# A two-layer hybrid decoder step on one core: constants split in two, the samples' last products reordered, identity products placed in waits

## The reference, cut to what matters

```python
def trunk(x, states, hist_valid, weights):
    for layer in range(DEPTH):          # DEPTH = 2
        if layer % 2 == 0:
            h, dconv, delta, pool = delta_pool_mixer(x, ...)   # "mixer 0"
        else:
            h, lconv, lru = rglru_mixer(x, ...)                # "mixer 1", the second mixer
        x = layer_norm(ALPHA * x + h, ln_mix_g[layer], ln_mix_b[layer])
        f = moe(x, router_w, router_bias, moe_w_gate[layer], moe_w_up[layer], moe_w_down[layer])
        x = layer_norm(ALPHA * x + f, ln_ffn_g[layer], ln_ffn_b[layer])

def gated_delta_rule(q, k, v, g, beta, s0):   # per head, in chunks of C rows
    m = jnp.where(strict, jnp.einsum('bhnid,bhnjd->bhnij', kb, k) * decay, 0.0)
    tinv = jnp.eye(C) - m;  power = -m
    for _ in range(max((C - 1).bit_length() - 1, 0)):
        power = power @ power
        tinv = tinv + tinv @ power
    ...
    # o = q_dec @ s + a_intra @ u_new,  s = s * exp(g_last) + k_dec^T @ u_new

# then: o = o * rsqrt(mean(o*o) + eps) * norm_w * silu(z);  y = concat(o, pooled) @ w_out
```

## Time and profile before

| | us |
|---|---|
| median of 3 runs | 1407.63 (1405.7 to 1408.05) |
| profiled execution | 1408.48 |
| its span, first to last instruction | 1406.7 |
| TensorE busy | 1244.5 (88%) |
| VectorE busy | 968.3 (69%) |
| ScalarE busy | 730.8 (52%) |
| GpSimdE busy | 183.6 (13%) |
| mean granted clock of TensorE | 0.935 |

### The profile page before, as it was taken

How to read it: one execution, slowest core, us unless ns; L and a number is a source line. 1 busy time by engine, 2 the same in 40 slices (tenths; PEclk the granted TensorE clock), 3 DMA queues, 4 the chain that set the end, 5 groups by cost and what they waited for, 6 DMA issues and landing times.

```text
span 1406.7 us, 18287 instructions
## 1 busy us (share of the span) xinstructions
PE 1244.5 (88%) x6605; PEld 1008.7 (72%) x6605; DVE 968.3 (69%) x1441; ACT 730.8 (52%) x1011; POOL 183.6 (13%) x251
## 2 busy tenths in 40 slices
PE   4999988889999699999999289998987999999970
PEld 3988887777445588888888189964456888888860
DVE  3766355441534599999997553738656999999957
ACT  2543242221101388888886553256133888888844
POOL 4011442200300010000000300031001100000002
PEclk9999999996899699999999599999987999999995
DMA  6211051001242689999994822030545899999835
GB/s 204 61 61 60 1 191 33 1 1 53 86 183 90 233 331 403 417 417 405 419 408 147 255 85 91 1 150 1 198 173 220 340 408 420 411 417 403 350 109 198
DMA packets 63102, 296.61 MB, mean 211 GB/s; under 512 B 6624, under 2 KB 32969, under 8 KB 50752
## 3 DMA queue, kind: packets, MB, share of 16 engines
q1 hardware_dynamic: 51136, 252.78, 46.6%
q0 software_dynamic: 7296, 26.22, 5.2%
q10 hardware_dynamic: 4608, 16.78, 3.0%
HBM read 268.87 MB, written 26.89 MB: 210 GB/s over the span
## 4 chain that ended last, share of the span: by engine, by line
PE 83%; DVE 9%; ACT 2%; issue 2%; POOL 2%; DMA 2%; POOLq 0%; DVEq 0%; ACTq 0%
PE bank L1067 24%; PE bank L1094 12%; PE bank L977 6%; PE bank L622 5%; PE bank L623 4%; PE bank L648 4%; PE bank L650 4%; PE bank L964 2%; PE bank L1014 2%; PE bank L1057 2%; PE bank L1223 2%; PE bank L988 2%; PE bank L609 1%; PE bank L718 1%; PE bank L1085 1%
## 5 line engine op out<-in xcount | busy, mean ns | idle before, releaser
L1248 ACT ACTIVATE GU_HIGH<-work 128x1024 fp32r<-128x1024 f32 x256 | 270.2, 1060 | 63.3 <-PE bank L1067 59.2
L1067 PE MATMUL bank<-GU_HIGH,XGT_HIGH 128*128 128x512 f32 x512 | 203.0, 397 | 6.1 <-DVE XGT_LOW_B L2206 6.1
L2012 DVE TENSOR_TENSOR WGT_LOW<-work,GU_HIGH 128x1024 fp32r<-128x1024 f32 x128 | 155.5, 1223 | 13.4 <-ACT GU_HIGH L1248 5.5
L1248 ACT ACTIVATE WDN_HIGH<-work 128x1024 fp32r<-128x1024 f32 x128 | 135.4, 1063 | 44.2 <-PE bank L1094 44.2
L2012 DVE TENSOR_TENSOR WUP_LOW<-work,GU_HIGH 128x1024 fp32r<-128x1024 f32 x128 | 153.1, 1222 | 7.3 <-ACT GU_HIGH L1248 3.1
L2228 DVE TENSOR_TENSOR WDN_LOW<-work,WDN_HIGH 128x1024 fp32r<-128x1024 f32 x128 | 151.7, 1221 | 7.6 <-ACT WDN_HIGH L1248 3.7
L1067 PEld LDWEIGHTS bank<-GU_HIGH,XGT_HIGH 128*128 128x128 f32 x512 | 96.9, 189 | 26.0 <-DVE XGT_LOW_B L2206 6.9
L1248 ACT ACTIVATE work<-bank 128x512 f32<-128x512 f32 (+5 forms) x124 | 53.4, 469 | 115.1 <-PE bank L711 26.9
L1248 ACT ACTIVATE W_HIGH<-work 128x1024 fp32r<-128x1024 f32 x36 | 37.8, 1058 | 129.6 <-PE bank L623 80.0
L1067 PE MATMUL bank<-GU_HIGH,XGT_LOW_A 128*128 128x512 f32 x256 | 100.6, 393 | 0.0
L1067 PE MATMUL bank<-WGT_LOW,XGT_HIGH 128*128 128x512 f32 x256 | 100.2, 391 | 0.0
(11 more groups left out here) (479 smaller groups left out, 2903.9 us busy)
## 6 DMA issues: line engine op xcount, KB each, us to landing
work<-in_moe_w_gate_dram SPq DMA_DIRECT2D x32, 2048.0 KB, 10.7
work<-in_moe_w_up_dram SPq DMA_DIRECT2D x32, 2048.0 KB, 10.5
work<-in_moe_w_down_dram SPq DMA_DIRECT2D x32, 2048.0 KB, 9.7
y_rows<-work ACTq DMA_DIRECT2D x32, 512.0 KB
work<-in_ab_w_in_dram SPq DMA_DIRECT2D x10, 1024.0 KB, 5.5
work<-in_c_w_in_dram SPq DMA_DIRECT2D x8, 1024.0 KB, 5.9
...
```

What stands on the lines that cost most here:

```text
L1067: last = mm(psum, x, w, start=(k == m == 0), stop=(k == KD - 1 and m == 2))
L1248: return nc.scalar.activation(out, in_, ACT.Copy, scale=scale)
L2012: V.tensor_tensor(low[u][:, 2 * n:2 * n + 2, :], w[u][:, 2 * n:2 * n + 2, :], high, ALU.subtract)\
```

## The change

1. `constants()` is cut in three. The identity is written first and raises `ident_ready`; then come the constants that ScalarE, VectorE and SyncE need early, which raise `consts_ready`, and GpSimdE's two small DMAs of gate parameters; then the masks and selectors, which raise the new `masks_ready`. TensorE's first transposes wait for the input and `ident_ready` alone; VectorE waits for `masks_ready` ahead of its first convolution, TensorE ahead of its first use of a selector (in the fourth block of the projection).
2. SyncE issues the first weight block `W0[0]` ahead of the histories, and the router's two tables behind the weight blocks.
3. Identity products (`keep_warm`, now with the bank as an argument) stand in the last prompt chunk (3 each at four places), in the samples' ladder (4, 1, 2, 3, 4 and 3) and at the start of the second mixer (14, then 8 behind each of the first three tiles' transposes, after a new wait for the first tile of the norm).
4. At the end of the samples' stage `root_spread(2)` comes ahead of `state_update(3)` on TensorE, and `new_states(3)` comes last on VectorE.

```diff
--- before.py
+++ after.py
@@ -299,7 +299,7 @@
-consts_ready = sem("consts_ready")
+ident_ready, consts_ready, masks_ready = sem("ident_ready"), sem("consts_ready"), sem("masks_ready")
 xt_ps, xt_lo, xt_hi = sem("xt_ps"), sem("xt_lo"), sem("xt_hi")
@@ -520,10 +520,9 @@
     load_x(X_IN)
-    sp.dma_start(rw[:, :, :], router_w.rearrange("(k p) e -> p k e", p=P)).then_inc(router_in, 16)
-    sp.dma_start(rbias[:, :], router_bias.partition_broadcast(P)).then_inc(router_in, 16)
     win = ab_w_in[0].rearrange("(k p) c -> p k c", p=P)
     sp.dma_start(wab_in, win[:, :, 2048:2056]).then_inc(wab_sem, 16)
+    sp.dma_start(W0[0], win[:, :, 0:256]).then_inc(w_in[0], 16)
     sp.dma_start(chist_rows[0:24, :], state_delta_conv[0].rearrange("s j c -> (s j) c")).then_inc(hist_in, 16)
@@ -534,12 +533,15 @@
             sp.wait_ge(proj_ps, 2 * (n - 4) + 2)
-        sp.dma_start(W0[n % 4], win[:, :, c:c + 256]).then_inc(w_in[n % 4], 16)
+        if n:
+            sp.dma_start(W0[n % 4], win[:, :, c:c + 256]).then_inc(w_in[n % 4], 16)
         if n == 3:
...
                   .then_inc(lists_zeroed, 16)
+    sp.dma_start(rw[:, :, :], router_w.rearrange("(k p) e -> p k e", p=P)).then_inc(router_in, 16)
+    sp.dma_start(rbias[:, :], router_bias.partition_broadcast(P)).then_inc(router_in, 16)
     sp.wait_ge(proj_ps, NPROJ)
@@ -598,7 +600,7 @@
                 pe.wait_ge(x_in, 32)
-                pe.wait_ge(consts_ready, 1)
+                pe.wait_ge(ident_ready, 1)
             if n == 3 and t == 0:
@@ -729,16 +731,23 @@
         d_pe.end(last, b, "y")
+        last_chunk = b == NT - 2
+        if last_chunk:
+            keep_warm(3, 0)
         d_act.wait(pe, b, "tb")
...
         d_pe.end(last, b, "x6")
+        if last_chunk:
+            keep_warm(3, 0)
         d_dve.wait(pe, b, "tt6")
...
         d_pe.end(last, b, "nw")
-        if b + 1 < NT - 1:
+        if last_chunk:
+            keep_warm(3, 0)
+        else:
             power_transposed(b + 1)
@@ -785,6 +796,7 @@
         e_pe.end(last, 0, "pt")
+        keep_warm(4, 0)
         pw, pwt = (Pa, Pb), (PTa, PTb)
@@ -801,15 +813,18 @@
                 e_pe.end(last, 0, f"pt{r}")
+            keep_warm(1 if r == 1 else 3, 0)
             e_dve.wait(pe, 0, f"p{r}")
...
             e_pe.end(last, 0, f"x{r}")
+            keep_warm(2 if r == 1 else 4, 0)
         e_dve.wait(pe, 0, "tt2")
...
         e_pe.end(last, 0, "nw")
+        keep_warm(3, 0)
         e_act.wait(pe, 0, "nw")
@@ -883,8 +898,8 @@
         out_part(0, 0, (NH + 3,), False, False)
+        root_spread(2)
         state_update(3)
-        root_spread(2)
         root_spread(3)
@@ -914,6 +929,7 @@
                 if n == 0:
+                    pe.wait_ge(masks_ready, 1)
                     pe.wait_ge(rows_ready, 1)
@@ -1045,10 +1061,10 @@
-    def keep_warm(n):
+    def keep_warm(n, b=6):
         for _ in range(n):
-            mm(bank[6][:, 0:P], ident[:, :], ident[:, :], start=True, stop=True)
+            mm(bank[b][:, 0:P], ident[:, :], ident[:, :], start=True, stop=True)
@@ -1197,7 +1213,11 @@
         pe.wait_ge(hist_out, 3 + 3)
-        to_channels(2, (0, 1, 2))
+        pe.wait_ge(norm_sum, NT + 1)
+        keep_warm(14, 3)
+        for t in range(3):
+            to_channels(2, (t,))
+            keep_warm(8, 3)
         split.wait(pe, 0, "x2")
@@ -1903,9 +1923,9 @@
         normed(1)
-        new_states(3)
         normed(2)
         normed(3)
+        new_states(3)
@@ -1948,6 +1968,7 @@
         gates()
+        dve.wait_ge(masks_ready, 1)
         dve.wait_ge(hist_out, 3)
@@ -2405,23 +2426,32 @@
     def constants():
-        for m, v in ((ident, 0.0), (ones, 1.0), (m_strict_bd, -1.0), (m_strict_off, -1.0), (m_strict_s, -1.0),
-                     (m_incl, 1.0), (m_incl_s, 1.0), (m_before, 1.0), (own_sample, 1.0), (ms_col, 0.0),
-                     (m_lower4, 1.0), (sel_gc, 0.0), (sel_row, 0.0), (sum_col, 0.0), (COL, 0.0), (scores, 0.5)):
+        do(G.memset(ident[:], 0.0))
+        G.affine_select(out=ident[:, :], in_=ident[:, :], compare_op=ALU.not_equal, fill=1.0, base=0,
+                        pattern=[[-1, P]], channel_multiplier=1).then_inc(ident_ready, 1)
+        mine(G.memset(wab, 0.0))
+        for m, v in ((ones, 1.0), (COL, 0.0), (scores, 0.5)):
             mine(G.memset(m[:], v))
...
         mine(G.memset(keep, 1.0))
-        mine(G.memset(wab, 0.0))
         mine(G.memset(U[:, :, 0:HIST], 0.0))
...
             mine(G.memset(buf[:, 0:CONV - 1], 0.0))
+        do(G.iota(iota_i[:, :], pattern=[[1, 16]], base=1, channel_multiplier=0))
+        do(G.tensor_copy(inv_cnt[:, :], iota_i[:, :]))
+        mine(G.memset(keep[:, 0:TP].rearrange("p (c l) -> p c l", l=P)[:, :, 0], 0.0))
+        do(G.memset(keep[:, TP:T].rearrange("p (c l) -> p c l", l=LS)[:, :, 0], 0.0))
         do(G.iota(tok_id[:, :], pattern=[[P, NT]], base=0, channel_multiplier=1))
-        mine(G.memset(keep[:, 0:TP].rearrange("p (c l) -> p c l", l=P)[:, :, 0], 0.0))
-        mine(G.memset(keep[:, TP:T].rearrange("p (c l) -> p c l", l=LS)[:, :, 0], 0.0))
-        keep_where(ident[:, :], [[-1, P]], 0, 1, 1.0, ALU.not_equal)
-
+        G.tensor_copy(tok_f[:, :], tok_id[:, :]).then_inc(consts_ready, 1)
+        for n, src in enumerate((a_dt_bias, a_log_decay)):
+            pool.dma_start(gpar[32:36, n:n + 1], src.rearrange("o h -> h o")).then_inc(gates_in, 16)
+        for m, v in ((m_strict_bd, -1.0), (m_strict_off, -1.0), (m_strict_s, -1.0),
+                     (m_incl, 1.0), (m_incl_s, 1.0), (m_before, 1.0), (own_sample, 1.0), (ms_col, 0.0),
+                     (m_lower4, 1.0), (sel_gc, 0.0), (sel_row, 0.0), (sum_col, 0.0)):
+            mine(G.memset(m[:], v))
+        mine.settle()
         keep_where(m_strict_bd[:, :], [[-1, P]], -1, 1)
@@ -2445,16 +2475,13 @@
         keep_where(sum_col[:, :, :], [[1, 8], [-1, 8]], 0, 0, 1.0, ALU.not_equal)
-        do(G.tensor_copy(tok_f[:, :], tok_id[:, :]))
         do(G.iota(slot_no[:, :].bitcast(I32), pattern=[[1, P]], base=0, channel_multiplier=0))
...
         do(G.tensor_copy(iota16[:, :], iota_i[:, :]))
-        do(G.iota(iota_i[:, :], pattern=[[1, 16]], base=1, channel_multiplier=0))
         mine(G.tensor_copy(before16[:, :], m_before[:, :]))
-        mine(G.tensor_copy(ones16[:, :], ones[:, :]))
         mine.settle()
-        G.tensor_copy(inv_cnt[:, :], iota_i[:, :]).then_inc(consts_ready, 1)
+        G.tensor_copy(ones16[:, :], ones[:, :]).then_inc(masks_ready, 1)
@@ -2489,8 +2516,6 @@
     def mixer0():
-        for n, src in enumerate((a_dt_bias, a_log_decay)):
-            pool.dma_start(gpar[32:36, n:n + 1], src.rearrange("o h -> h o")).then_inc(gates_in, 16)
         for c in range(NCHUNK):
...
```

## The result

The changed kernel took 1400.83 us (median of 5 runs, 1397.78 to 1401.22) beside 1408.05 us (5 runs) for the kernel before; the ratio is 0.9946, with a 95% interval from 0.9926 to 0.9966. That is 7.2 us faster, where 13.6 were forecast, and the median lies just outside the range of 1389 to 1400 us. Its profiled execution took 1401.22 us with a span of 1399.5.

A forecast was written before the change was run, and what follows sets the result against it. TensorE, 83% of the chain of waits, was taken as the bound; 5.0 + 0 + 1.0 + 4.4 + 3.2 + 0 = 13.6 us off the profiled 1408.48 gave 1394.9, median 1394.0, own range 1390 to 1398 us (0.72).

The forecast's parts named there:

- Start: First transposes wait for the input, not GpSimdE's last constant: 5.0 us saved, bounds 1.5 to 5.5.
- Last chunk: Twelve identity products in the last prompt chunk hide in TensorE's waits: 0 us, bounds 0 and 1.6 lost.
- Samples' powers and thin products: Seventeen identity products hold the clock: 1.0 us saved in the powers, 4.4 in the 16-column products behind them.
- My lower bound: Samples' powers: 2.9 us lost if the clock falls all the same and the identity products run at half pace.
- the bound of 0 for L820: 16-column products: nothing of the forecast 4.4 us saved if the clock is lost before them; upper bound 6.9.
- rival A: Identity products don't hold the clock: 5.3 us saved in all, 1402.3 us; chance 0.10.
- End of the samples' stage: Fourth spread no longer waits for VectorE's new states: 3.2 us saved, 2.1 at the low clock, upper bound 5.
- Second mixer: Identity products ahead of its projection, whose start VectorE's chain sets: 0 us, bounds 1.9 saved and 2.4 lost.
- B: At the start the histories land late and 3.5 us of the gain are gone: 1397.5 us; chance 0.08.
- C: Second mixer's identity products run at half pace and delay it by 2.4 us: 1396.4 us; chance 0.06.
- D: Clock falls in the prompt chunks, 6.7 us each; three lost chunks make it slower, 1414 us; chance 0.03.

The follow-up runs named there:

- p2_warm: Kernel before with only the identity products of the last prompt chunk (twelve) and the samples' powers (seventeen) added; 1407.15 us, ratio 0.9997.
- q2_all_chunks: Changed kernel with the last chunk's twelve identity products in all four prompt chunks; 1398.68 us, ratio 0.9933 against the kernel before.
- p1_front: Kernel before with only the split constants and the new order of the first transfers; 1401.16 us, ratio 0.9961.
- p3_end: Kernel before with only the new order at the end of the samples' stage; 1403.65 us, ratio 0.9987.
- r1_no_powers: Changed kernel without the seventeen identity products of the samples' powers, the last chunk's kept; 1397.49 us, ratio 0.9927 against the kernel before.
- q1_again: Changed kernel run again, unaltered; 1400.77 us, ratio 0.9954 against the kernel before.
- s2_plain: Changed kernel without any of its identity products: split constants, transfer order and reordered end only; 1399.87 us, ratio 0.9945 against the kernel before.

## Why the prediction was wrong

**Start, 5.0 us: right.** Alone it measured 5.5 (2.8 to 8.2). It went as said: the input decides, the histories are not late, the masks neither. In the profile 5.7 us shrank to 2.7 by the last chunk. The low clock under the transposes took 1.3 of it, which was nearly made up by the start of the projection (5.3), and 5.4 still stood at 185 us; the two chance stretches at 187 and 218 us took the other 2.7.

**Last chunk, 0: right.** From L740 to L797 the lead doesn't change.

**Samples' powers and thin products, 1.0 + 4.4 us: this is the step that failed.** It measured 0.4 us, between 3.0 faster and 2.3 slower (p2_warm). The mechanism is there: in six of the seven profiles that have the seventeen products and unmoved mean squares, the clock holds until 3.3 to 3.8 us into the thin products, and these take 10.2 to 10.6 us; in the seventh, q2_all_chunks, it holds 1.5 us and they take 12.3. Three things were mis-sized. The clock held 3.5 us into them, not 4.4, so 3.4 us and not 4.4. In the ladder I put 1.2 us against the products and 2.2 for the clock; it came out 0.2 us longer than in the profile of before, and the products cost 2.0 against a ladder at the full clock. These two leave 3.4 us of the 5.4, measured against the profile of before. And I took the profile of before for what the kernel does, where it showed a ladder in which the clock had fallen; I priced the gain against that case alone. Other profiles (p1_front, p3_end, r1_no_powers) keep the clock nearly through the ladder with no product in it, and there nothing is gained (56.5 us without them and 56.4 to 56.8 with; 58.8 and 58.8 with the old end). My lower bound (2.9 us lost with the clock) and the bound of 0 for L820 held this, but I gave them 0.10 as rival A, which spoke of products that don't hold the clock; they hold it, and the gain is missing all the same. That case stood in none of the rivals.

**End of the samples' stage, 3.2 us: right in kind, too large.** From the table it is 2.3 us between profiles in which the clock fell alike (62.14 to 59.8, 58.80 to 56.5), near the 2.1 given for a spread at the low clock, and alone it measured 1.8 (-0.1 to 3.8). That products of four rows carry the clock no better, no run shows: it fell at 371.6 under L878, in the kernel before at 378.0 in a wait, and the mean-square products, whose output has four rows, are where it came back.

**Second mixer, 0: right.** Alone 1.1 us slower, within what can't be told; TensorE waits for the split as before.

**Rivals.** A and B didn't come, C neither. D did in small: the clock fell twice in the first chunk in the profiled execution, worth 2.7 us (q1_again, without them, is 0.5 us ahead of the first profile at 185 us and 3.2 at 225), where the rival spoke of whole chunks and of 6.7 us each. My argument against it, that all four chunks kept the clock, was one execution's. What the page of the Trainium skill says (TensorE: Matmul & The Clock Gate, Part 1), that the moment of a change of level differs between runs, is what these runs show: within one kernel, the falls at 187 and 218 us of the first profile are in neither of the two later ones, and the same ladder has the fall 2.6 us behind its start in one kernel's profile (s2_plain) and 6.0 us in another's (r1_no_powers). The other rule, that long idle gaps cost the clock (HAM oscillation), I set aside for this place, where the longest wait was 0.92 us; at the expert's gate the runs agree with it in kind, though the wait is shorter than the gaps that the section gives: 2.50 us idle, then the fall, and no fall with 0.49. (In the profile of before the clock stayed up behind that wait in the first layer and fell in the second.) I looked at four places for the clock and not at that wait.

**The sum.** 5.0 + 5.4 + 3.2 was forecast, 5.5 + 0.4 + 1.8 measured, and 1.1 lost in the second mixer: 6.6 us, and the whole 7.2.
